# Linear attention's output norm: squares summed onto every partition by one product with ones, root and reciprocal on 128x1024 values

## The reference

```python
GLA_HEADS, GLA_VALUE_DIM, SEQ = 4, 128, 256
def rmsnorm(x, gain):
    y = xf * lax.rsqrt(jnp.mean(xf * xf, axis=-1, keepdims=True) + RMS_EPS)
    return (y * gain).astype(x.dtype)
# at the end of gla_branch, o is (B, S, H, DV)
o = rmsnorm(o, out_gain).reshape(B, S, H * DV)
return o * jax.nn.silu(og)
```

## Time and profile before

| what | value |
|---|---|
| median of the runs | 1118.33 us |
| profiled execution, its own time | 1118.4 us |
| its span, first to last instruction | 1116.6 us |
| PE busy | 1092.6 us, 98% |
| DVE busy | 572.4 us, 51% |
| ACT busy | 465.6 us, 42% |
| HBM read | 311.16 MB, 280 GB/s over the span |

### The profile page before, as it was taken

One profiled execution on the slowest core, in us unless ns is written; L12 is line 12 of the kernel. 1 busy time (PEld: TensorE's weight loads), 2 busy tenths in 40 slices (PEclk: granted clock), 3 DMA queues, 4 the chain that ended last, 5 costly groups with the idle time before them and its releaser, 6 DMA issues.

```text
span 1116.6 us, 14331 instructions
## 1 busy us (share of the span) xinstructions
PE 1092.6 (98%) x5822; PEld 755.3 (68%) x5822; DVE 572.4 (51%) x906; ACT 465.6 (42%) x746; POOL 0.2 (0%) x4
## 2 busy tenths in 40 slices
PE   8999999999999999999999999999999999999997
PEld 6998888888886344434379988888888753444432
DVE  6669574656565123323277686745575642323222
ACT  5677565566543001010166856755655420010000
POOL 0000000000000000000000000000000000000000
PEclk9999999999999999999999999999999999999999
DMA  9545454263777999999964344452449699999995
GB/s 373 225 151 187 148 191 154 76 226 151 285 294 311 430 427 428 427 427 428 420 258 181 128 183 151 151 191 92 171 154 368 247 370 430 427 427 428 427 427 247
DMA packets 23955, 313.14 MB, mean 280 GB/s; under 512 B 3153, under 2 KB 3281, under 8 KB 5457
## 3 DMA queue, kind: packets, MB, share of 16 engines
q1 hardware_dynamic: 23616, 312.22, 69.8%
q10 hardware_dynamic: 272, 0.00, 0.0%
HBM read 311.16 MB, written 1.05 MB: 280 GB/s over the span
## 4 chain that ended last, share of the span: by engine, by line
PE 87%; DMA 6%; DVE 4%; ACT 2%; issue 1%; DVEq 0%; SPq 0%
PE slot L639 35%; PE M L971 16%; PE slot L1004 9%; PE slot L622 8%; DMA arena<-in_w_up 6%; PE slot L865 3%; PE slot L930 2%; PE slot L568 2%; PE M L823 1%; PE slot L943 1%; PE M L801 1%; PE M L943 1%; PE M L772 1%; PE M L812 1%; PE M L746 1%
## 5 line engine op out<-in xcount | busy, mean ns | idle before, releaser
L1402 DVE TENSOR_TENSOR w_lo<-ring,w_hi 128x1024 fp32r<-128x1024 f32 x199 | 239.4, 1223 | 153.6 <-ACT w_hi L1061 152.1
L1061 ACT ACTIVATE w_hi<-ring 128x1024 fp32r<-128x1024 f32 x200 | 208.2, 1055 | 102.2 <-PE slot L639 70.6
L639 PE MATMUL slot<-w_hi,hT_hi 128*128 128x512 f32 x480 | 192.5, 401 | 0.0
L639 PE MATMUL slot<-w_lo,hT_hi 128*128 128x512 f32 x480 | 187.3, 390 | 0.0
L639 PE MATMUL slot<-w_hi,hT_lo 128*128 128x512 f32 x480 | 187.0, 390 | 0.0
L1835 DVE TENSOR_TENSOR arena<-arena,M 128x512 f32<-128x512 f32 x16 | 11.0, 688 | 203.4 <-PE M L971 203.4
L639 PEld LDWEIGHTS slot<-w_lo,hT_hi 128*128 128x128 f32 x480 | 90.1, 188 | 19.4
L639 PEld LDWEIGHTS slot<-w_hi,hT_hi 128*128 128x128 f32 x480 | 90.2, 188 | 18.8 <-issue 0.8
L639 PEld LDWEIGHTS slot<-w_hi,hT_lo 128*128 128x128 f32 x480 | 90.3, 188 | 18.1 <-issue 0.5
L622 PE MATMUL slot<-hT_hi,w_hi 128*128 128x256 f32 x256 | 73.4, 287 | 0.0
L622 PE MATMUL slot<-hT_hi,w_lo 128*128 128x256 f32 x256 | 72.4, 283 | 0.0
(11 more groups left out here) (278 smaller groups left out, 1650.2 us busy)
## 6 DMA issues: line engine op xcount, KB each, us to landing
ring<-in_w_mix SPq DMA_DIRECT2D x48, 2048.0 KB, 8.2
ring<-in_w_down SPq DMA_DIRECT2D x18, 2048.0 KB, 19.7
arena<-in_w_gate SPq DMA_DIRECT2D x12, 2048.0 KB, 18.8
ring_down<-in_w_gate SPq DMA_DIRECT2D x12, 2048.0 KB, 20.3
ring<-in_w_up SPq DMA_DIRECT2D x10, 2048.0 KB, 19.8
ring_up<-in_w_up SPq DMA_DIRECT2D x6, 2048.0 KB, 16.8
ring_odd<-in_w_up SPq DMA_DIRECT2D x6, 2048.0 KB, 21.0
arena<-in_w_up SPq DMA_DIRECT2D x6, 2048.0 KB, 22.4
```

The lines of the kernel that those rows point to most:

```text
L639: last = mm(o[:, t * 512:(t + 1) * 512], h[:, 2 * n + cc, t * P:(t + 1) * P], w[:, cc * 512:(cc + 1) * 512], start=n == cc == k == 0, stop ...
L1061: A(piece_of(w_hi, i), source(i), ACT.Copy).then_inc(hi_ready.sem, 1)
L1402: v.tensor_tensor(piece_of(w_lo, i), source(i), piece_of(w_hi, i), ALU.subtract)\
```

## The change

The eight products with the column of 1/128 become two products of `ones` with `gsq` itself, at the same place of TensorE's program (after job J_K). `M0` then has the sum of squares of each head and token on every partition, 128x1024 values. ScalarE takes the root of all of them, with a scale of 1/128, into `gsq`. The diagonal blocks and the second product (after J_K+1) go. VectorE takes the reciprocal of 128x1024 values, in place in `gsq`, between L1584 and L1589, and L1589 reads `gsq` instead of `M0`. The constant column of 1/128 and two semaphores go as well.

```diff
                 pe.wait_ge(go_sq.sem, go_sq.at(l, 1))
-                for b in range(NT * HG):
-                    last = mm(M0[:, b:b + 1], gsq[:, b * P:(b + 1) * P], c("mean"), start=True, stop=True)
+                for i in range(2):
+                    last = mm(M0[:, i * 512:(i + 1) * 512], ones, gsq[:, i * 512:(i + 1) * 512],
+                              start=True, stop=True)
                 last.then_inc(gmean_ps.sem, 1)
...
                 time_major(J_K + 1)
-                pe.wait_ge(gdiag_ready.sem, gdiag_ready.at(l, 1))
-                for i in range(2):
-                    last = mm(M0[:, i * 512:(i + 1) * 512], ones, gsq[:, i * 512:(i + 1) * 512],
-                              start=True, stop=True)
-                last.then_inc(grinv_ps.sem, 1)
                 for u, j in enumerate(range(J_K + 2, J_G)):
...
                 act.wait_ge(gmean_ps.sem, gmean_ps.at(l, 1))
-                A(grinv, M0[:, 0:NT * HG], ACT.Sqrt, bias=eps).then_inc(grms.sem, 1)
+                A(gsq, M0[:, :], ACT.Sqrt, bias=eps, scale=1.0 / DV).then_inc(grms.sem, 1)
                 qk_stats(3)
...
                 split_ahead(J_K, PIECES)
-                dve.wait_ge(grms.sem, grms.at(l, 1))
-                link(v.reciprocal(grinv, grinv))
-                v.tensor_tensor(gsq.rearrange("p (b t) -> p b t", b=NT * HG),
-                                ident.unsqueeze(1).broadcast_to((P, NT * HG, P)),
-                                grinv.unsqueeze(2).broadcast_to((P, NT * HG, P)), ALU.mult).then_inc(gdiag_ready.sem, 1)
                 qk_norm(3)
                 split_ahead(J_K + 1, PIECES)
...
                 link(w)
-                dve.wait_ge(grinv_ps.sem, grinv_ps.at(l, 1))
+                dve.wait_ge(grms.sem, grms.at(l, 1))
+                link(v.reciprocal(gsq, gsq))
                 for hh in range(2):
-                    w = v.tensor_tensor(by_half(br[0], hh), from_half(M0, hh), by_half(og, hh), ALU.mult)
+                    w = v.tensor_tensor(by_half(br[0], hh), from_half(gsq, hh), by_half(og, hh), ALU.mult)
                 w.then_inc(brA_ready.sem, 1)
```

More of the change, by code:

```diff
@@ L136 @@
 CONST, NCONST = columns([
-    ("ident", P), ("freq", ROPE), ("eps", 1), ("mean", 1), ("ones", P), ("before", P), ("gla_mask", P),
+    ("ident", P), ("freq", ROPE), ("eps", 1), ("ones", P), ("before", P), ("gla_mask", P),
     ("band", NPAT * T), ("iota", T + CAP), ("caps", NPASS), ("key4", NG), ("key16", NE),
@@ L279, in build @@
         asum, arinv = small[:, 14:22], small[:, 30:38]
-        grinv = small[:, 85:93]
         asd = (small[:, 22:30], small[:, 76:84])
@@ L323, in build @@
         go_ps, go_sq, gmean_ps, grms = Signal("go_ps", 1), Signal("go_sq", 1), Signal("gmean_ps", 1), Signal("grms", 1)
-        gdiag_ready, grinv_ps = Signal("gdiag_ready", 1), Signal("grinv_ps", 1)
         brA_ready = Signal("brA_ready", 1)
@@ L1880, in constants @@
     put("ident", i == j)
-    put("mean", 1.0 / P)
     put("ones", 1.0)
```

## The result

The changed kernel takes 1128.76 us (median of six runs, 1127.80 to 1129.53) against 1118.35 us before (1118.09 to 1118.98): ratio 1.0094, 95% interval 1.0083 to 1.0104. It is 10.4 us slower. The forecast was 1124.5 us with a range of 1121.5 to 1129.8. The profiled execution is one of the slower ones, 1129.33 us with a span of 1127.6, so its trace has 11.0 us of span to explain.

A forecast was written before the change was run, and what follows sets the result against it. TensorE, busy 98% of the span, was taken to bound the kernel. A loss of 3.03 us in each of two layers, TensorE's saving included, added 6.1 us to 1118.4: 1124.5 us, range 1121.5 to 1129.8.

The forecast's parts named there:

- TensorE's saving: Around J_K+1, one wide product replaces the eight small ones and another group goes: 1.81 us a layer, 3.6 in all.
- The root on ScalarE and `qk_norm(3)` later at no cost: ScalarE's root grows to 1.01 us, +0.75; qk_norm(3) on VectorE starts 0.75 later, at 137.9, within a slack of 1.8 us.
- The reciprocal: VectorE's new 128x1024 reciprocal before L1589: 6.3 us at 6.0 ns for each element, bounds 1.2 and 8.0 us.
- the eight steps: Rival: VectorE's reciprocal takes eight plain steps for each element, 8.7 us, total 1129.2 us; chance 0.14.
- Which waits end up on TensorE: TensorE idles 1.5 us before J_K+2's transposes and 3.3 us before J_V, which starts at 162.18, 3.03 us late.
- The formula: Loss in a layer at J_V's start is the reciprocal's time less 3.27 us.
- the short reciprocal: Rival: VectorE's reciprocal streams near the plain rate, 1.2 to 1.5 us, TensorE never waits, total 1114.8 us; chance 0.07.
- No second wait, nothing given back: After J_V's late first quarter TensorE waits no more, and no later idle time in the mixer wins the loss back.
- The clock: TensorE's clock stays up through 3.3 us idle before J_V, as through the longest earlier wait, 3.0 us at the start.
- the likeliest case: Forecast of 1124.5 us, chance 0.63; a reciprocal of 5.5 to 7.0 us gives 1122.9 to 1125.9.
- The rival that said so: Idle before J_V drops TensorE to 1.2 GHz for a quarter of a job: +5.4 us, total 1129.9; chance 0.10.
- the prediction's own sign of being wrong: The prediction is wrong if a granted clock below full appears in the slice of J_V.
- Row 12: Profile row cited for TensorE's longest earlier wait, 3.0 us at the very start, after which the clock stayed up.

The follow-up runs named there:

- e4: The changed kernel without its reciprocal of 128x1024, output used as a measure only: 1114.47 us, ratio 0.9958 against the kernel before.
- e7: The kernel before with one unused reciprocal of 128x512 added on VectorE ahead of L1589: 1118.79 us, ratio 1.0003.
- e3: The kernel before with one unused reciprocal of 128x1024 added on VectorE ahead of L1589: median 1136.06 us with three long executions, 1129.62 us when run again.
- e6: The changed kernel with the first two w_lo quarters of J_V formed ahead of qk_norm(4): 1118.56 us, ratio 1.0003.
- e1: The changed kernel with filler products in TensorE's waits: 1125.24 us with 6 before the transposes and 11 before J_V, 1125.02 us with only the 11.
- e2: The changed kernel with the w_lo of J_V's first quarter formed ahead of qk_norm(4): 1121.69 us, ratio 1.0023.

## Why the prediction was right, and where not

- **TensorE's saving**, 1.81 us a layer: right. e4 gives 3.7 for the two layers where 3.6 was worked out from the spacing of matmul starts.
- **The root on ScalarE and `qk_norm(3)` later at no cost**: right. 1.11 us instead of the 1.01 taken from the square; `qk_norm(3)` at 137.76 against 137.9 predicted.
- **The reciprocal**: 6.55 us against 6.3. The two lengths give (6553 - 3345) / 512 = 6.27 ns for each element, above the 6.0 of the short rows, far below the eight steps of 8.3. The slope of rows with 1 to 8 elements held to 5% at 1024. That term was 0.25 us a layer too small, 0.5 in all. The choice of 6.0 among slopes of 5.5, 5.7 and 6.0 had little ground, and that a slope from 8 elements holds to 1024 was a guess that came out; no row of before could tell. The rivals of the short reciprocal and of eight steps fell with it.
- **Which waits end up on TensorE**: right in place and size. 1.5 and 3.3 us predicted, 1.68 and 3.06 measured; J_V's start 162.18 predicted, 162.25 measured, which is 162.48 on the clock of the execution before (0.23 us behind, as above). The 0.3 is nearly all the reciprocal's. The formula, the reciprocal less 3.27 us, gives 3.28 with the measured 6.55; the trace has 3.33, and e7 shows that about the first 3.1 us are free.
- **No second wait, nothing given back**: right; from J_V+1 to the end of the span the lag hardly changes but for layer 1's own loss.
- **The clock**: here the likeliest case failed. It held that TensorE would come through 3.3 us of idle time at 2.4 GHz, on the ground of the one wait of 3.0 us at the start of the kernel before, through which "the clock stayed up". The runs showed 1.2 GHz in both layers (4.2 us in the trace, 3.5 to 3.7 between the medians with and without fillers). The rival that said so had 1 chance in 10, a size of 5.4 us where the trace has 4.2, and a total of 1129.9; the prediction's own sign of being wrong, a granted clock below full at J_V, came true.

The ground itself was misread. L531's products of the kernel before, first in the first 9 us of the program and then in layer 1 (nanoseconds, shortest/median/longest; PEld is the weight load), and the weight loads of the changed kernel's J_V in layer 1 while its granted clock reads 0.50:

```profile
L531 PEld LDWEIGHTS M<-cst x22: 288/333/338, 3.0 to 8.3; 128*128 128x128 f32 x22
L531 PE MATMUL M<-cst x22: 421/421/582, 3.0 to 8.5; 128*128 128x128 f32 x22
...
L531 PEld LDWEIGHTS M<-cst x18: 186/192/192, 559.2 to 566.0; 128*128 128x128 f32 x18
L531 PE MATMUL M<-cst x18: 270/275/377, 559.4 to 566.1; 128*128 128x128 f32 x18
...
L637 PEld LDWEIGHTS slot<-w_hi,hT_lo x5: 330/330/333, 719.3 to 724.4; 128*128 128x128 f32 x5
```

After the wait at the start a weight load takes 333 ns and a product 421, where the same line takes 192 and 275 later; 330 is what a load takes at 0.50. So TensorE worked at the durations of the lower level for 5.5 us behind that wait, though the granted clock of those slices reads full. Row 12 was no case of a clock that survives 3 us of waiting. Whether that wait brought the clock down or the program began with it down, no run separates. The durations were in the trace of before, and with them the rival deserved far more than 1 in 10.

The total, 1128.76 us, lies inside the stated range only because the range took in part of the clock; the likeliest case alone reached from 1122.9 to 1125.9.

Between the medians: waits 6.7 and clock 3.5 to 3.7 make 10.2 to 10.4 of the 10.4 us. What decides how long the lower clock lasts (a loss of 1.4 to 1.6 us or of 2.8 to 2.9) was not tried.

## What to carry to other kernels

Put a price on each element of the operation that a change widens, also on the engine that is half idle: trading a small reciprocal and a second product for one wide reciprocal moved 6.5 us onto VectorE to save 1.8 on TensorE. Whether that costs is read from what is queued behind it in the same engine's order and from the slack of the first waiter; here about the first 3.1 us were free, and the same work in two pieces at the engine's idle places, with the waited-for quarter moved ahead, was free entirely. When the sum leaves TensorE an idle stretch of about 3 us, add the loss of clock behind it as a likely term, and if the wait can't be removed, try filler products, which got that part back here. Where the clock through an earlier wait is to serve as evidence, compare the durations of the same instruction behind it and elsewhere, and not the granted clock alone.

## What the hardware did that I had not expected

- The reciprocal of float32 on VectorE takes 6.27 ns for each element of the free dimension (128x512 3.35 us, 128x1024 6.55), six times an operation on two tensors (1.04 ns).
- One idle stretch of TensorE of 3.06 us, with full work before it, brought its clock from 2.4 to 1.2 GHz in e3 and in the changed kernel, in both layers. Stretches of 1.68 us (e6), of 1.73 us (e1), and of 1.68 and 1.36 us with 4.7 us of work between them (e2) did not.
- Behind the wait of 3.0 us at the start of the program, weight loads take 333 ns instead of 192 and products 421 instead of 275 until 8.5 us, while the granted clock reads 1.00.
- The lower clock outlasted the wait by 3 us in one layer and by nearly 6 in the other, though TensorE was busy without a break from J_V's start on; which layer has the longer stretch changes from one execution to the next.
